# Queries, keys and convolution pieces turned in 32x32 blocks by VectorE and moved by ScalarE, in place of 112 transposes on TensorE

## What is computed

```python
# layer 1: x + mix(rms_norm(x)) @ w_out, then the gated FFN
qa, ka, va, ra, ga, qb, kb, vb = split(h @ w_in)
out_a = gla_mixer(qa, ka, va, ra, gates(ga))          # 4 heads, chunks of 64
out_b = dilated_mixer(rms_norm(qb), rms_norm(kb), vb) # 8 heads of 128
x = x + concat(out_a, out_b) @ w_out
x = x + (silu(h2 @ w_gate) * (h2 @ w_up)) @ w_down
# layer 2, even mixer: retention beside a gated convolution of 3 taps
q, k, v, g_ret, gate_b, gate_c, u, g_conv = split(h @ ev_w_in)
ret_out = rms_norm(retention(rope(q), rope(k), v)) * silu(g_ret)
conv_out = gate_b * conv(gate_c * u) * silu(g_conv)
x = x + concat(ret_out, conv_out) @ ev_w_out
# layer 2, odd mixer: attention in a window, heads of 64
x = x + (attention(...) * silu(gate)) @ od_w_out
```

## Time and profile before

| | |
|---|---|
| median of 3 runs | 1936.26 us (1936.25 to 1936.84) |
| profiled execution, its own time | 1936.57 us |
| its span | 1934.8 us |
| granted clock of TensorE | 1.000 |
| TensorE busy | 1927.6 us, 100% |
| VectorE busy | 1207.6 us, 62% |
| ScalarE busy | 933.0 us, 48% |
| GpSimd busy | 14.4 us, 1% |
| DMA queue of the weights | 350.66 MB, 59.4% of 16 engines |

### The profile page before, as it was taken

One profiled execution on the slowest core, in us unless ns is written; L12 is line 12 of the kernel. 1 busy time (PEld: TensorE's weight loads), 2 busy tenths in 40 slices (PEclk: granted clock), 3 DMA queues, 4 the chain that ended last, 5 costly groups with the idle time before them and its releaser, 6 DMA issues.

```text
span 1934.8 us, 22606 instructions
## 1 busy us (share of the span) xinstructions
PE 1927.6 (100%) x8935; PEld 1587.8 (82%) x8935; DVE 1207.6 (62%) x1743; ACT 933.0 (48%) x1234; POOL 14.4 (1%) x32
## 2 busy tenths in 40 slices
PE   9999999999999999999999999999999999999999
PEld 7888887888888888888888888888888888888887
DVE  6655466766666456665466766545655666677775
ACT  6545454554444344443444554444444455556653
POOL 0001000000000000000000000000000000000000
PEclk9999999999999999999999999999999999999999
DMA  9666664566665666666666566665566556545445
GB/s 307 199 185 149 179 179 142 169 179 195 195 193 192 194 192 189 196 195 195 195 192 193 187 191 185 195 190 166 166 192 190 188 182 185 158 149 151 144 144 169
DMA packets 183560, 354.85 MB, mean 183 GB/s; under 512 B 11472, under 2 KB 12288, under 8 KB 183456
## 3 DMA queue, kind: packets, MB, share of 16 engines
q1 hardware_dynamic: 182208, 350.66, 59.4%
q0 software_dynamic: 816, 2.11, 0.9%
q10 hardware_dynamic: 432, 0.66, 0.1%
HBM read 351.27 MB, written 2.11 MB: 183 GB/s over the span
## 4 chain that ended last, share of the span: by engine, by line
PE 99%; DMA 1%; DVE 0%; ACT 0%; SPq 0%; issue 0%; DVEq 0%
PE g L908 31%; PE g L910 31%; PE g L909 30%; PE m L842 2%; PE m L986 1%; PE ob L1004 0%; PE ob L1003 0%; PE ob L1002 0%; DMA raw<-in_w_in 0%; PE m L978 0%; PE m L976 0%; DMA A<-in_xT 0%; PE m L1068 0%; PE ob L1057 0%; PE ob L1051 0%; PE m L1039 0%
## 5 line engine op out<-in xcount | busy, mean ns | idle before, releaser
L1366 DVE TENSOR_TENSOR wl<-raw,wh 128x1024 fp32r<-128x1024 f32 (+1 forms) x660 | 802.9, 1217 | 629.6 <-ACT wh L1109 626.8
L1109 ACT ACTIVATE wh<-raw 128x1024 fp32r<-128x1024 f32 (+1 forms) x661 | 696.8, 1055 | 775.8 <-PE g L910 771.0
L908 PE MATMUL g<-wh,xh 128*128 128x512 f32 x1886 | 745.2, 395 | 2.3 <-DVE xl L1369 1.5
L910 PE MATMUL g<-wh,xl 128*128 128x512 f32 x1886 | 735.2, 390 | 0.0
L909 PE MATMUL g<-wl,xh 128*128 128x512 f32 x1886 | 734.1, 389 | 0.0
L908 PEld LDWEIGHTS g<-wh,xh 128*128 128x128 f32 x1886 | 354.2, 188 | 80.1 <-issue 8.2
L910 PEld LDWEIGHTS g<-wh,xl 128*128 128x128 f32 x1886 | 354.0, 188 | 75.0
L909 PEld LDWEIGHTS g<-wl,xh 128*128 128x128 f32 x1886 | 354.5, 188 | 70.5
L908 PE MATMUL g<-wh,mh 128*128 128x512 f32 x732 | 289.2, 395 | 0.0
L910 PE MATMUL g<-wh,ml 128*128 128x512 f32 x732 | 285.3, 390 | 0.0
L909 PE MATMUL g<-wl,mh 128*128 128x512 f32 x732 | 285.1, 389 | 0.0
(11 more groups left out here) (144 smaller groups left out, 785.2 us busy)
## 6 DMA issues: line engine op xcount, KB each, us to landing
raw<-in_ev_w_in SPq DMA_DIRECT2D x128, 512.0 KB, 3.7
raw<-in_w_in SPq DMA_DIRECT2D x92, 512.0 KB, 4.3
raw<-in_w_gate SPq DMA_DIRECT2D x88, 512.0 KB, 4.3
raw<-in_w_up SPq DMA_DIRECT2D x88, 512.0 KB, 3.8
raw<-in_w_down SPq DMA_DIRECT2D x88, 512.0 KB, 4.7
raw<-in_od_w_in SPq DMA_DIRECT2D x72, 512.0 KB, 3.6
raw<-in_w_out SPq DMA_DIRECT2D x32, 512.0 KB, 3.8
raw<-in_ev_w_out SPq DMA_DIRECT2D x32, 512.0 KB, 3.9
```

What stands on the lines that cost most here:

```text
L908: e.matmul(o, hi[:, kt, c], h, start=first, stop=False)
L910: last = e.matmul(o, lo[:, kt, c], h, start=False, stop=end)
L1109: return e.activation(o, i, AF.Copy, scale=scale)
L1366: return e.tensor_tensor(o, a, b, op)
```

## The change

`turned_by_blocks` says one `flip` and four `move`. `flip` is one VectorE transpose of 128x1024 that transposes each 32x32 block of `W0` (or of `cc`) within its place, into `W1`. Each `move` is four ScalarE copies of 32 partitions by 2x4x32 columns, one for each quarter of the source's partitions, into the quarter of partitions `b` of the destination; a gain goes with the copy of qk, for which `qg` and `kg` grow from one column to four. So 14 blocks get 14 transposes of 128x1024 and 14 x 16 = 224 copies; 28 x 4 transposes on TensorE and 28 evacuations of 128x512 go. The convolution's last factor is now read from `cgT` in SBUF (`cg_mul`) instead of a bank. Writers of `W1` wait until all moves said before them are done (`flip_free`). `conv` moves to the lane `fin`. And the lane `post` is now a queue: a block's work is appended and waits for the one before it, where `launch` drained it; a guard says the evacuation of the block two places back before a block's first matmul.

```diff
@@ lay
+            while un.first and b.i >= 2 and b.i - 2 not in self.emptied:
+                self.step()
...
-                    self.launch("post", self.after(b))
+                    self.lanes["post"].append(self.after(b))
+                    if len(self.lanes["post"]) == 1:
+                        self.advance("post")
@@ after
             say("qk_evac", key, j, b.i)
-            for p in ("qk_sq", "qk_sum", "qk_root", "qk_norm"):
-                yield 1 if (b.i, p) == (0, "qk_sq") else 2
+            for p, n in (("qk_sq", 1), ("qk_sum", 2), ("qk_root", 1), ("qk_norm", 2)):
+                yield n
                 say(p, key, j)
-            yield 3 if b.i else 2
-            for k in range(2):
-                say("qk_turn", key, j, k)
-                yield 1
+            yield 1
+            yield from self.turned_by_blocks("qk", key, j)
+            yield 1
...
+    def turned_by_blocks(self, kind, key, j):
+
+        self.say("flip", kind, key, j)
+        for b in range(4):
+            yield 2 if b else 1
+            self.say("move", kind, key, j, b)
@@ scalar
+                        on.wait_ge(*flip_free(p))
                     act(W1, W0, AF.Square).then_inc(s_qk_sq, 1)
-                elif kind == "qk_turn":
...
+                elif kind == "move":
+                    which, key, j, b = a
+                    on.wait_ge(*flipped(which, key, j))
...
+                    for q in range(4):
+                        here, there = slice(32 * q, 32 * q + 32), slice(32 * b, 32 * b + 32)
+                        gain = C(key + "g", b, b + 1)[here, :] if which == "qk" else 1.0
+                        last = copy(dst[there, :, :, 32 * q:32 * q + 32],
+                                    W1.rearrange("p (k c n) -> p k c n", k=2, c=4)[here, :, :, 32 * b:32 * b + 32],
+                                    gain)
+                    last.then_inc(s_move, 1)
@@ vector
+                elif kind == "flip":
...
+                    e.transpose(W1, src).then_inc(s_flip, 1)
...
-                elif kind == "cg_turn":
+                elif kind == "cg_mul":
                     j, h = a
+                    on.wait_ge(*in_place("cg", 0, j))
+                    on.wait_ge(s_conv, 4 * j + 4)
                     y2 = yc[:, 2 * h:2 * h + 2, :]
...
+                    tt(y2, cgT[:, 2 * h:2 * h + 2, :], y2, ALU.mult).then_inc(s_cg_mul, 1)
```

More of the change, by code:

```diff
@@ L148, in say @@
             self.norms += 1
+        if p[0] in EMPTIED_BY_ACT + EMPTIED_BY_DVE:
+            self.emptied.add(p[-1])
     def advance(self, lane):
@@ L258, in after @@
             say("ta_evac", a[0], b.i)
[L259 to L262, removed]
+            yield 2
+            yield from self.turned_by_blocks("ta", a[0], 0)
         elif kind in ("va", "sr", "gate", "rv", "cc", "cb"):
@@ L284, in after @@
                 yield 2
[L285 to L288, removed]
+            yield from self.turned_by_blocks("eq", key, j)
         elif kind == "gret":
@@ L296, in after @@
             say("cu", j, b.i)
-            yield 2
+            yield 1
             say("cz", j)
[L299 to L305, removed]
+            yield from self.turned_by_blocks("cu", 0, j)
+            self.launch("fin", self.convolution(j))
         elif kind == "cg":
@@ L334, in after, with convolution @@
             self.lanes["att"].append(self.od_heads(a[0]))
+    def turned_by_blocks(self, kind, key, j):
[3 more added lines that the diff above has]
+            self.say("move", kind, key, j, b)
+    def convolution(self, j):
+        for c in range(4):
+            yield 1 if c == 0 else 3
+            self.say("conv", j, c)
     def od_norm(self, x):
@@ L553, in program @@
     ropes = {p: n + 1 for n, p in enumerate(q for q in plan.order if q[0] == "eq_rope")}
+    flips = {p: n + 1 for n, p in enumerate(q for q in plan.order if q[0] == "flip")}
+    moves = {p: n + 1 for n, p in enumerate(q for q in plan.order if q[0] == "move")}
     def last_unit(acts):
@@ L671, in split_free, with flipped, in_place, flip_free @@
             return (s_mul, last_unit(f"{kind}{i - 1}") + 1) if i else (s_mul, 0)
+        def flipped(kind, key, j):
+            return s_flip, flips[("flip", kind, key, j)]
+        def in_place(kind, key, j):
+            return s_move, moves[("move", kind, key, j, 3)]
+        def flip_free(p):
+            before = [q for q in plan.order[:plan.order.index(p)] if q[0] == "move"]
+            return s_move, len(before)
         def normed(acts):
@@ L1180, in scalar @@
                     if n > 1:
-                        before = [q for q in plan.order if q[0] == "qk_turn" and q[-1] == 1][n - 2]
-                        on.wait_ge(*full(*before))
+                        on.wait_ge(s_flip, n - 1)
                     evacuate(T3, b)
@@ L1265, in scalar @@
                     on.wait_ge(*normed("X2"))
[L1266 to L1277 removed]
+                    on.wait_ge(s_flip, flips[("flip", "eq", key, j)] - 1)
+                    evacuate(T3, b)
                 elif kind == "rv":
```

149 lines of the change are left out of this document (69 added, 80 removed).

## The result

The changed kernel takes **1939.99 us** (20 runs) beside 1936.72 for the kernel before (20 runs on the same chip). The ratio is 1.0017 with a 95% interval of 1.0010 to 1.0024: slower by some 3.3 us. Forecast were 1925.2 us, with a range of 1923.4 to 1930.0, and 0.90 for faster. Size and sign are both wrong. One of the 20 runs of each kernel took several times as long as the rest; it is left out of the ratio and does not move a median. The profiled execution took 1940.04 us, with a span of 1938.2.

What follows compares the result with a forecast made beforehand. TensorE, busy 1927.6 of 1934.8 us, was taken as the bound. 1936.57 - 12.4 (transposes) + 0.4 + 0.65 (norms) + 0.3 (convolution) = 1925.5, or 1925.2 us against the runs' median; range 1923.4 to 1930.

Steps and rivals of the forecast that it cites:

- What goes: TensorE: 28 groups of four transposes at 0.446 us leave the path, 12.5 us, taken as 12.4.
- VectorE's transposes: VectorE: 14 new transposes of 128x1024, 1.24 us each.
- The working of a qk block up to its first move: ScalarE and VectorE, queries and keys: cut, evacuation, square, sum, root, norm, transpose; copies start 13.75 us after the cut's earliest start.
- The price of a queued copy: ScalarE's 224 copies: 0.41 us queued with a gain, 0.32 without; bounds 0.27 and 0.60; ScalarE keeps up narrowly.
- The evacuation and square behind them leave 1.1 again. No stall: Query and key blocks: after four groups of copies, evacuation and square leave 1.1 us of reserve, so TensorE does not stall.
- the 2.86 us of reserve: Weights feeding TensorE: 5.18 us from a cut's earliest start to its unit, 2.32 used; added work below 2.86 is free.
- Norms: First norm ahead of the gate stalls 0.4 us; last layer's norm 0.4 plus 0.25 for the key's sum and root.
- Convolution beside the retention: First cu block: four groups of 1.3 us on ScalarE against 0.79 us of reserve; 0.3 us of stall.
- retention's queries and keys: The eq blocks, two ropes ahead of the transpose: copies start at 11.25, leaving 1.2 us of reserve; no cost.
- (a): Rival: dear ScalarE copies between cuts in all 14 blocks, deciding above 0.49 us each; about 1944 us; 0.05 that it ends slower.
- The signs to look for: Trace checks, including ScalarE copy means of 0.40 to 0.50 us; wrong if starts exceed 0.49 apart or L908 waits for wl.

Runs made afterwards that it cites:

- e_norm_drain: Changed kernel with lane post drained only where one block of the residual sum follows another: 1938.58 us.
- e_pool_rest: Changed kernel with the moves without gain issued by GpSimd; those of queries and keys stay on ScalarE: 1937.34 us.
- e_best: Changed kernel with late query/key moves and own square place, post drained between residual-sum blocks, other moves on GpSimd: 1924.28 us beside 1936.74, ratio 0.9936.
- e_late2: Changed kernel, query/key square in its own place, moves in their own lane and later, last two groups behind the next block's sum: 1928.10 us beside 1937.08.
- e_loop_open: Changed kernel with the query/key square in a place of its own and the moves in a lane of their own: 1945.09 us.
- e_copies: Changed kernel plus a series of test copies on ScalarE, VectorE and GpSimd behind the last output; some 60 us longer expected.

## Why the prediction was wrong, step by step

- **What goes: right.** 12.4 us forecast, 12.5 by the starts. The 275 ns of the Trainium skill, TensorE: Matmul & The Clock Gate, section PE-mode transpose, would as a price have been wrong by a factor of 2.5; they are a duration, as the row's 272 are.
- **VectorE's transposes: right**, 1.24 us forecast, 1238 ns.
- **The working of a qk block up to its first move: right.** Forecast 13.75 us from the cut's start, measured 13.72 (91.40 to 105.12).
- **The price of a queued copy: mis-sized.** 0.41 and 0.32 us forecast, 0.52 and 0.425 measured, within the bounds of 0.27 to 0.60. I took the overlap of 0.1 us from copies that all begin at partition 0 to moves that each begin at another partition than the instruction ahead. With the cut's own lost overlap a group is 3.17 us, not 2.6, against 2.72: ScalarE does not keep up.
- **"The evacuation and square behind them leave 1.1 again. No stall": the step that failed.** I followed one block from a full reserve and did not ask when the next could begin. On my own numbers the fourth group is done 13.75 + 1.64 + 3 x 2.6 = 23.2 us after the first cut, and the next evacuation starts one cut later, at 24.15, which is 23.2 us after this one at 0.96, against 21.76: a drift of 1.4 us per block, which after two blocks has used up the 2.86 us of reserve. At a copy of 0.425 us the run without gains stalled 6.1 us in this stretch; at 0.52 the changed kernel stalled 12.2. The rows of the order ahead of the prediction end with the fourth group of moves, and so did my working: I asked what the moves wait for, not what stands behind them.
- **Norms: right in place, mis-sized.** 1.05 us forecast, 1.4 measured by `e_norm_drain`.
- **Convolution beside the retention: 0.3 forecast, 1.55**, and retention's queries and keys 0 forecast, 1.0 measured. Both go for the most part with ScalarE's copies (2.65 us in `e_pool_rest`). The trace that I had for this stretch showed 0.79 us of reserve, too little for four groups that each add 0.1 (2.81 against the 2.72 of a unit) behind a wait.
- **Rivals.** (a) had the right sign, place and cause of a kind ("dear copies between cuts", decided above 0.49; the copy of queries and keys is 0.52), and I gave it 0.05. But its formula has the same fault: at 0.52 it gives 16 x 0.52 - 5.28 = 3.0 us against a reserve of 2.5 to 3.5 and so next to no stall, where 12.2 came. The rule of the Trainium skill, VectorE: DVE Perf Modes, section Rules for kernel authors (leave a 128x128 transpose to TensorE where its output may be in PSUM) agrees with the kernel as changed, and not with `e_best`, which turns by blocks and is 12.5 us faster than the kernel before.
- **The signs to look for** were well chosen in part: "L908 waits for `wl` inside the qk blocks" and "starts over 0.49 us apart" are what came.

The stated time, 1925.2, lies between `e_late2` (1928.10, only the queries and keys reordered) and `e_best` (1924.28, the norms and the other moves mended too). It was a forecast for a schedule that the changed kernel does not have; that it comes so near `e_best`, whose moves are partly on another engine, is chance.

## What to carry to other kernels

For a chain that repeats, work out its period, not only whether one turn of it fits the reserve: from an instruction to the same instruction of the next block, through every queue in program order, also where no semaphore is set between the two. If that is over what the bounding engine needs for the block, every block pays the difference. And a price of a queued instruction is read from starts, with the first partitions and the neighbours that it will have; a mean duration hides 0.1 us in 0.4.

A move that waits should stand in its engine's order where it is due, and the next block's evacuation ahead of what is not urgent: that took 12 us here, with as many instructions of the same kinds. (The square needs a place of its own for it, since it stands ahead of moves that still read the old one; that place without the order, `e_loop_open`, gained nothing.)

## What the runs showed that I had not expected

- In these traces an instruction of ScalarE begins some 0.1 us before the end of the one ahead only if it reads and writes from the same first partitions. Copies of 32 partitions that change them start 0.427 us apart, copies of 128 partitions of the same 256 columns 0.307, with means of 415 and 401 ns; a cut takes 1.08 ahead of a copy that writes from partition 32 on and 0.96 ahead of one that stays at partition 0. VectorE's copies in `e_copies` look alike: 0.297 apart with changing quarters, 0.201 with all 128 partitions, for 0.284 and 0.288 us each.
- GpSimd: 0.435 us from start to start for a plain 32x256 copy alone. Beside the other engines' work it takes 0.39 to 0.44 us, or 1.27 to 1.47 if one of VectorE's subtractions is running when it starts (42 of 42, and none of the 118 others, in `e_pool_rest`). With a multiplication by a column it takes 0.92 and 1.3 to 2.9.
- Draining a lane, harmless before, cost 5.7 us at one place once the lane held moves.
